# A two-block network on one core: the first block's small attention over the memory put ahead of the local one, the decays of the recurrence moved inside the attention, and v centred per head where its group norm was centred before

## The reference, cut to what matters

```python
h = rms_norm(x, norm_g)
p = h @ w_in                      # all operands of the three branches, and the gates
# branch a, a recurrence over time (8 heads of 64), with per-channel decays w and a:
#   every projection is mixed with its value one token earlier: u + mu * (u_prev - u)
#   kk = normalised k;  bonus = (sum over the head of r*k*r_k) * v
#   y = group_norm_per_head(recurrence(r, w, k, v, kk, a)) + bonus
# branch b, local attention with sinks: q, k are rms-normed per head, then rotated (rope)
# branch c, attention over 256 memory tokens: q and k rms-normed per head of 128
y_a, y_b, y_c = y * silu(z_a), local(...) * silu(z_b), cross(...) * silu(z_c)
merged = sigmoid(g0) * (y_a @ w_proj_a) + sigmoid(g1) * (y_b @ w_proj_b) + sigmoid(g2) * (y_c @ w_proj_c)
x = x + merged @ w_out
```

## Time and profile before

| | before |
|---|---|
| median of 3 runs | 1932.92 us (1932.4 to 1935.56) |
| profiled execution, its own time | 1931.05 us |
| span of its records | 1928.9 us |
| TensorE busy | 1783.4 us (92%) |
| VectorE, ScalarE, GpSimd busy | 712.4, 422.1, 136.2 us |
| mean granted clock of TensorE | 0.968 |

### The profile page before, as it was taken

How to read it: one execution, slowest core, us unless ns; L and a number is a source line. 1 busy time by engine, 2 the same in 40 slices (tenths; PEclk the granted TensorE clock), 3 DMA queues, 4 the chain that set the end, 5 groups by cost and what they waited for, 6 DMA issues and landing times.

```text
span 1928.9 us, 20481 instructions
## 1 busy us (share of the span) xinstructions
PE 1783.4 (92%) x8040; PEld 909.8 (47%) x8040; DVE 712.4 (37%) x1456; ACT 422.1 (22%) x800; POOL 136.2 (7%) x124
## 2 busy tenths in 40 slices
PE   5998789996799999999999979999999999999997
PEld 3643334452355555544454457644644444444443
DVE  3006434445533333322438988521424222221012
ACT  4022533343211111020215322400301111111000
POOL 0002120000000100000006700000000000000001
PEclk8999899998899999999999979999999999999998
DMA  4311011110001111112221112122012222221121
GB/s 181 107 66 44 33 55 44 55 44 33 33 34 35 34 34 34 34 55 95 76 76 66 66 55 66 45 77 72 27 66 77 76 76 77 76 76 66 66 87 65
DMA packets 34159, 119.75 MB, mean 62 GB/s; under 512 B 3792, under 2 KB 4048, under 8 KB 33680
## 3 DMA queue, kind: packets, MB, share of 16 engines
q1 hardware_dynamic: 32976, 113.79, 17.4%
q10 hardware_dynamic: 864, 3.35, 0.4%
q0 software_dynamic: 224, 1.31, 0.2%
HBM read 116.34 MB, written 2.10 MB: 61 GB/s over the span
## 4 chain that ended last, share of the span: by engine, by line
PE 78%; DVE 12%; issue 5%; ACT 4%; DMA 1%; POOL 0%; ACTq 0%; DVEq 0%; POOLq 0%
PE bank L462 55%; PE vpair L582 3%; PE bank L888 3%; DVE arena L1291 3%; PE bank L478 2%; PE bank L512 2%; PE opair L606 2%; DVE tmp L1282 2%; PE abank L697 2%; DVE arena L1707 2%; PE abank L555 1%; PE vpair L697 1%; DVE max L1706 1%; PE bank L487 1%; PE vpair L566 1%
## 5 line engine op out<-in xcount | busy, mean ns | idle before, releaser
L462 PE MATMUL bank<-h,ring 128*128 128x512 f32 x1840 | 835.0, 605 | 24.3 <-ACT tmp L997 14.6
L462 PEld LDWEIGHTS bank<-h,ring 128*128 128x128 f32 x1840 | 346.3, 193 | 437.2 <-issue 404.0
L462 PE MATMUL bank<-arena,ring 128*128 128x512 f32 (+1 forms) x992 | 406.0, 563 | 14.0 <-ACT arena L980 8.2
L462 PEld LDWEIGHTS bank<-arena,ring 128*128 128x128 f32 x992 | 187.8, 194 | 209.8 <-issue 184.9
L1291 DVE SCALAR_TENSOR_TENSOR x<-bank,x 128x512 f32<-128x512 f32 x32 | 22.1, 692 | 260.0 <-PE bank L462 216.7
L1291 DVE SCALAR_TENSOR_TENSOR arena<-arena,cols 128x512 f32<-128x512 f32 x125 | 94.0, 752 | 4.4
L1282 DVE TENSOR_TENSOR arena<-arena,vpair 128x256 f32<-128x256 f32 x87 | 36.6, 421 | 156.1 <-PE vpair L697 109.9
L980 ACT ACTIVATE arena<-bank 128x512 f32<-128x512 f32 (+1 forms) x67 | 34.7, 518 | 269.2 <-PE bank L462 211.1
L1285 DVE TENSOR_SCALAR arena<-arena,cols 128x512 f32<-128x512 f32 x24 | 13.1, 546 | 206.8 <-ACT arena L1246 206.6
L582 PE MATMUL vpair<-arena 128*128 128x256 f32 (+4 forms) x224 | 72.1, 427 | 7.5 <-issue 4.3
L555 PE MATMUL abank<-sq,cst 128*128 128x512 f32 (+1 forms) x58 | 33.6, 720 | 44.8 <-ACT sq L952 37.5
(11 more groups left out here) (194 smaller groups left out, 1564.0 us busy)
## 6 DMA issues: line engine op xcount, KB each, us to landing
ring<-weights SPq DMA_DIRECT2D x201, 512.0 KB, 3.2
ring<-weights SPq DMA_DIRECT2D x16, 256.0 KB, 2.9
x<-xt SPq DMA_DIRECT2D x4, 512.0 KB, 7.6
out<-h SPq DMA_DIRECT2D x8, 256.0 KB, 2.1
cst<-cst_in ACTq DMA_DIRECT2D x1, 1504.0 KB, 14.2
arena<-memt ACTq DMA_DIRECT2D x1, 1024.0 KB, 7.8
arena<-mem2t POOLq DMA_DIRECT2D x1, 1024.0 KB, 5.1
tmp<-pos ACTq DMA_DIRECT2D x1, 256.0 KB, 10.3
```

Of the source, the lines that this page charges most:

```text
L462: last = mm(o[:, 0:n], weight(), src, start=c == 0, stop=c == len(srcs) - 1)
```

## The change

The order of the first layer's work changes, and one piece of arithmetic.

- Front: the memory attention's q and both of its norms come first, beside the groups of z_c; then q, k and v of the local attention with one norm for all five tiles; then the operand tile of the decays. The z_b groups leave the front.
- Attention: memory jobs first (steps 0 to 7), then the local ones (8 to 23). What was ahead of the attention or behind it is called inside it through the new table `inject` on TensorE, `before` on ScalarE and `after` on VectorE: rotations of q after steps 1 to 4, of k after 5 and 6, kk and the decays' rounds from step 13, at 13, 16, 19 and 22. The fills are 20 groups.
- `EARLY` and `LATE` are one list `GATES`; all eight tiles are filled into the recurrence, 12 pairs for each iteration.
- v is centred per head in each decay round (one more `single`, one more VectorE product), and the four `single`s and VectorE products behind the recurrence are gone.
- Buffers follow: the decays' scratch `E` lies in xq and km, the mean squares in bb and kk.

```diff
-        lwa = thz[:, 0]
-        E = [SP[:, 0], SP[:, 1], SP[:, 2], SP[:, 3], PT[:, 0], PT[:, 1]]
+        lwa = take(T)
+        E = [xq[:, 0], xq[:, 1], xq[:, 2], xq[:, 3], km2[:, 0], km2[:, 1]]
...
-        stage("attention operands", *[A8] * (8 + 10 + 8))
-        stage("recurrence operands", *[A8] * 17)
-        stage("gates early", *[A8, V4, A8, V4] * len(EARLY))
-        stage("gates late", *[A8, V4, A8, V4] * len(LATE))
+        stage("front operands", *[A8] * (8 + 4 + 4 + 4 + 2 + 1))
+        stage("attention fill", *[A8] * (4 + 4 + 8 + 4))
+        stage("gates", *[A8, V4, A8, V4] * len(GATES))
...
+        KK_AT = 13
+        DECAY_AT = (13, 16, 19, 22)
+        GATE_PAIRS = 12
...
                     fill(work, fills(i)[2])
+                    if i in inject:
+                        inject[i]()
...
+            dense(h)
+            norm_sums(con("ones"), 4, 1, M)
+            for n in range(2):
                 dense(h)
+            work = stream([hs] * 9)
+            fill(work, 4)
+            for i in range(2):
+                norm_sums(con("ones"), 2, 1, first=2 * i)
+                fill(work, 2)
+            finish(work)
             pe.wait_ge(cst_in.sem, 16)
+            work = dense_tokens_pairs(h, NT)
+            for i in range(5):
+                fill(work, 2)
+                norm_sums(con("head_ones"), 1, 1, first=i)
+            finish(work)
+            dense(h)
+            work = stream([hs] * 20)
...
+            def bonus_sum(i):
+
                 pe.wait_ge(rk_ready.sem, i + 1)
                 single("v", con("head_ones"), E[0])
+                single("v", con("head_ones"), v[:, i, :])
+
+            inject = {}
+            for i in range(4):
+                inject[1 + i] = lambda i=i: rotate_query(i)
+                inject[DECAY_AT[i]] = lambda i=i: decay_sums(i)
+                inject[DECAY_AT[i] + 2] = lambda i=i: bonus_sum(i)
+            for s in range(2):
+                inject[5 + s] = lambda s=s: rotate_key(s)
...
+            attention(memory_jobs() + window_jobs(), work, inject=inject)
...
-                    fill(work)
+                    if it == 0:
+                        pe.wait_ge(o_read.sem, gates_from)
+                    fill(work, 2)
...
-                    fill(work)
+                    fill(work, 2)
                     pe.wait_ge(wu_ready.sem, it + 1)
...
-                    fill(work, 2)
+                    fill(work, 3)
...
-            for i in range(4):
-                pe.wait_ge(lnx_ready.sem, 1)
-                single("v", con("head_ones"), rwy[:, i, :])
             work = stream([hs] * 8)
```

On VectorE the five norms of q and k now stand right ahead of the attention, and the rounds inside it:

```diff
+            for i in range(5):
+                ri = rinv_refined(i)
+                dst = memq[:, i, :] if i < 4 else skn
+                stt(dst, dst, col("q_g" if i < 4 else "k_g"), ri, MUL, MUL, norm_applied)
+                signal_now(rope_in)
...
+            def free_scores():
+
+                st["freed"] = st["att"]
+                dve.wait_ge(exp_done.sem, st["att"])
+                signal_now(v_read)
...
                 o = v_in()
                 tt(bonus[:, i, :], o[:, :], v[:, i, :], MUL, v_read)
+                o = v_in()
+                stt(v[:, i, :], o[:, :], -1.0 / HD, v[:, i, :], MUL, ADD, v_read)
                 signal_now(head_done)
...
+            for i in range(4):
+                after[1 + i] = lambda i=i: rope_between(lambda: rope(memq[:, i, :], memq[:, i, :]))
+                after[DECAY_AT[i] + 1] = lambda i=i: decay_sums(i)
+                after[DECAY_AT[i] + 2] = lambda i=i: decay_apply(i)
...
+            after[KK_AT + 1] = first_decay
+            after[10] = lambda: dve.wait_ge(silu_done.sem, 8)
+            shifted(0)
+            dve.wait_ge(silu_done.sem, 4)
+            attention(memory_jobs() + window_jobs(), FILL1, [None] * 4 + [lambda n=n: shifted(n) for n in range(1, 13)] + [None] * 4,
+                      after=after)
```

More of the change, by code:

```diff
@@ L317, in stage_groups @@
             return groups[start[name]:start[after]]
-        RECUR = stage_groups("recurrence operands", "gates early")
-        GEARLY = stage_groups("gates early", "gates late")
+        FILL1 = stage_groups("attention fill", "gates")
         CROSSKV = [(who, n or KD) for who, n in stage_groups("cross kv", "w_out_2")]
-        GLATE = stage_groups("gates late", "gates a")
+        GATED = stage_groups("gates", "gates a")
         nblocks = sum(n for _, n in groups)
@@ L545, in take_pair, with norm_sums @@
                 return vpair if kind == "v" else opair
-            def norm_sums(ones, norms, tiles, n=T):
+            def norm_sums(ones, norms, tiles, n=T, first=0):
                 for i in range(norms):
@@ L568, in _, with attention @@
             att = {"p": 0, "pt": 0}
-            def attention(jobs, work=iter(()), fills=even_fills):
+            def attention(jobs, work=iter(()), fills=even_fills, inject={}):
                 n = len(jobs)
-                v_before.append(state["v"])
+                v_of = []
+                v_of_jobs.append(v_of)
                 for i in range(n + 3):
@@ L662, in _ @@
+            inject[7] = rotated
+            assert KK_AT == DECAY_AT[0]
+            inject[KK_AT] = first_decay
+            pe.wait_ge(wa2_in.sem, 16)
+            attention(memory_jobs() + window_jobs(), work, inject=inject)
             finish(work)
-            work = stream([hs, ybs, hs, ycs] * len(LATE))
+            ybs, ycs = ([y[:, c, :] for c in range(4)] for y in (yb, yc))
+            work = stream([hs, ybs, hs, ycs] * len(GATES))
+            gates_from = state["o"]
             n_ml = n_xx = 0
@@ L1104, in _ @@
                 do(fn(gexp[:, i, 0:7], gexp[:, i, 0:7], ACT.Exp), exps_ready)
-                read_through(reading, GEARLY, 6 * i)
-            read_through(reading, GEARLY, 24)
+            before = {KK_AT: kk_squares}
+            for i in range(4):
+                before[DECAY_AT[i] + 1] = lambda i=i: decay_tanh(i)
+                before[DECAY_AT[i] + 2] = lambda i=i: decay_exps(i)
+            attention(memory_jobs() + window_jobs(), FILL1,
+                      [lambda n=n: silu_in(yb[:, n]) for n in range(4)] + [lambda n=n: raw_tile(n) for n in range(1, 13)] +
+                      [lambda n=n: silu_in(ya[:, n]) for n in range(4)], before=before)
             act.wait_ge(head_done.sem, 4)
-            reading = {"done": 0, "todo": [gate] * (2 * len(LATE))}
+            act.wait_ge(silu_done.sem, 12)
+            reading = {"done": 0, "todo": [gate] * (2 * len(GATES))}
             act.wait_ge(o_read.sem, 24)
@@ L1783, in do @@
                 pool.wait_ge(sig.sem, sig.n)
-            dst = [y[:, n] for y in (yb, yc, ya) for n in range(4)]
+            dst = [y[:, n] for y in (yc, yb, ya) for n in range(4)]
             for n in range(12):
```

220 lines of the change are left out of this document (103 added, 117 removed).

## The result

The changed kernel takes 1873.65 us (median of 4 runs, 1872.71 to 1874.93), the kernel before 1934.24 (4 runs, 1932.4 to 1935.66): a ratio of 0.9688, interval 0.9671 to 0.9704. The forecast was 1875. The profiled execution after took 1874.93, its span 1873.1.

The account below looks back on a forecast made before the run. Chains of dependent work were taken to hold TensorE in the front and the decays, with slow clock behind each wait. -89.8 up to the recurrence, +39.3 in it and -7.5 behind gave -58, so 1875 us, range 1854 to 1901.

Parts of the forecast that it names:

- Front: Before the attention: work, 6.5 us of waits and 2 for the clock put the attention's start at 186.5, against 245.1.
- Start of the attention: At the first rotation TensorE waits 5.5 us, since VectorE must refine five tiles first.
- Step 13: In the attention, sums of kk and decays wait 1.9 us for banks from behind ScalarE's load and Ln.
- Step 16: In the attention, the scores take the bonus sum's bank, queued behind VectorE's work from step 14: TensorE waits 4.7 us.
- Later rounds: Decay rounds after the first, without kk: fill groups' readings and the bonus bank come late by 1.9, 2.2 and 0.3 us.
- The attention's total: 224.7 us of work and old waits, new waits of 5.5 + 13.1, 4 for the clock: 247.3, ending at 433.8.
- Recurrence: 24 more pairs cost 41.3 us at clock 1.00, less 2 for waits covered between iterations: +39.3.
- Behind it: Behind the recurrence, four sums go and the first gate group starts at 814.7 instead of 822.35: -7.5 us.
- rounds not hidden: Rival, chance 0.24: in the attention TensorE waits for the half rounds, 49 us instead of 13 at worst; band 1887 to 1911.
- The waits mostly do not happen: Rival, chance 0.12: the 18.6 us of waits and 6 of clock shrink to a few, 1852.
- The gate pairs: Rival, chance 0.10: pairs fill the recurrence's 15.2 us that are not busy; it grows by 26 instead of 39, 1862.
- The rule weighed: ScalarE's table switch: the skill's 1283 ns load plus about 1380 ns drain would give 1878; the forecast took 1.28 us.

Follow-up runs that it names:

- silu_ahead: The changed kernel with ScalarE reading the first z_c group ahead of Ln and Exp of the memory q tiles instead of behind them: 1866.77 us, ratio 0.9666.
- refine_inside: The changed kernel with one tile refined ahead of the attention, the other four each behind the rotations of steps 1 to 4: 1870.75 us, ratio 0.9686.
- refine_spread: The changed kernel with refining inside the attention, the second tile before the first rotation, the others each behind the rotation after it: 1867.68 us, ratio 0.9664.
- reads_first: The changed kernel with VectorE reading the sums of bonus and v ahead of the four products in each round's second half: 1867.7 us, ratio 0.9665.
- centre_outputs: The changed kernel with v left uncentred and the outputs centred behind the recurrence again, by four sums and four products: 1873.07 us, ratio 0.9685.
- three_edits: The changed kernel with refine_inside, silu_ahead and later decay rounds (13, 17, 20, 23; second halves from step 16) together: 1860.23 us, ratio 0.9634.
- four_edits: The changed kernel with refine_spread, silu_ahead, reads_first and later decay rounds (13, 17, 20, 23; second halves from step 16) together: 1858.37 us, ratio 0.9613.
- gates_behind: The changed kernel with 9 pairs per recurrence iteration as before the change, the other 24 run in one piece behind it: 1875.36 us, ratio 0.9695.

## Why the prediction was right

The mechanism was the forecast one: chains that TensorE had stood behind now lie beside its work. That the total came within 1.4 us is luck in part, since larger errors cancel in it. By steps:

- **Front.** Forecast 186.5, measured 188.1. Waits for the sums of the memory keys 2.5 us (forecast 2.6), for the third z_c group 4.31 (3.9). The 1.6 over are slow clock, sized at 2 and about 3.6: the three groups at 82.87, behind the first waits, took 22.46 us where three at 6.95 take 20.85, and 2.0 lie behind the wait of 4.31, as silu_ahead shows. The waits add 0.3, and the work was priced 0.3 too high.
- **Start of the attention.** 6.53 (5.5) at the first rotation, behind the five tiles. refine_inside and refine_spread show the cause.
- **Step 13.** Forecast 1.9, measured next to nothing: the sums of kk at 306.04 have no idle time in front, and from there to the next pair at 312.57 TensorE takes about 0.8 us more than these products cost elsewhere, in small pieces. This term was wrong. The walk took ScalarE's load to begin behind the sums, as it stood at 432.06. In the trace after, the load comes first:

```profile
304.02 1.28 ACT L996 ACT_TABLE_LOAD   x1
...
307.10 0.69 ACT L996 ACTIVATE sq<-abank,cols 128x512 f32<-128x512 f32 x1 [1.80 <-PE abank L565]
...
310.68 1.28 ACT L998 ACT_TABLE_LOAD   x1
311.98 2.98 ACT L998 ACTIVATE sq<-sq,cols 128x512 f32<-128x512 f32 x4
```

- **Step 14.** 1.32 (1.0) for the transposes, 1.42 (1.1) for the pair behind them. Right.
- **Step 16.** 3.97 (4.7). VectorE of the kernel after:

```profile
331.98 0.69 DVE L1350 SCALAR_TENSOR_TENSOR arena<-arena 128x512 f32<-128x512 f32 x1
332.71 2.15 DVE L1341 TENSOR_TENSOR arena<-arena 128x512 f32<-128x512 f32 x3
334.89 0.69 DVE L1341 TENSOR_TENSOR arena<-vpair,arena 128x512 f32<-128x512 f32 x1
335.61 0.69 DVE L1350 SCALAR_TENSOR_TENSOR arena<-vpair,arena 128x512 f32<-128x512 f32 x1
```

  The scores start at 335.63, 0.05 us behind the end of the bonus reading (334.89 + 0.69). reads_first shows it by moving that reading.
- **Later rounds.** 1.96, 1.54 and nothing, for 1.9, 2.2 and 0.3.
- **The attention's total.** It is 244.3 us long for 247.3, and the recurrence starts at 432.4 for 433.8: -91.2 for -89.8. Three errors hide in this. The new waits sum to 16.7 for 18.6. The slow clock behind them cost 7.8 for 4: 2.8 behind the first rotation, 3.3 behind step 16 and 1.7 behind the wait of 1.54, by the records. And the 224.7 of "work and old waits" was between 5 and 6 too large: it kept 2.5 us of old waits (1.01, 1.05, 0.21 and 0.20) and about 3 of slow clock at the two ends of the old attention, and of such the new one has only a wait of 0.47, at 216.27.
- **Recurrence.** 335.4 for 330.4: the largest error. The 24 pairs cost 41.2, as sized. The 2 us of covered waits never came: TensorE's waits between iterations after are those of before, to the tenth.

```profile
PE abank L735 <- DVE arena L1341: 4.2, 8, 0.5
PE vpair L827 <- DVE arena L1341: 3.2, 3, 1.1
PE vpair L725 <- DVE tmp L1341: 1.8, 3, 0.6
```

  In the trace before the lines of the same three products read 4.2, 3.2 and 1.8. The other 3 us are clock (below), which the forecast had at 1.00.
- **Behind it.** -7.6 for -7.5, but not as worked out: the group begins right at the end of the recurrence, and the price of the centring inside the attention was undersized. The working said that "its four VectorE products stand behind the bonus bank's release, so only head_done is later". It left out that its sum takes a bank of its own from the pool that the scores draw on. centre_outputs measures 9.2 us in the attention, not 3.6. Part of that was in the sum under another name: the 4.7 and 2.2 of score waits, put down to the bonus bank, are there only because the second sum shifts the scores onto it. Without them the fill pairs wait longer for ScalarE (5.1 us in rounds where the kernel after has 1.96 beside 5.5 of score waits), so that 2.4 of the 9.2 are waits, 3.6 the sums, and the rest mostly slow clock.
- **Rest.** 1093.5, unchanged within 1.2 us of before.

The errors of +1.6 in front, -3.0 in the attention, +4.9 in the recurrence, -0.1 behind it and -1.2 in the rest sum to +2.2; the profiled execution took 1874.93 for 1873. The median is nearer to the forecast's 1875 than that says, since it lies 1.3 below the profiled execution, where it was put 1.9 above; that is luck.

The rivals: rounds not hidden (1887 to 1911) needs waits over 6 us at each of the four rounds; none is over 4, and it falls. "The waits mostly do not happen" falls too, but three_edits and four_edits show what it would have been: 1860 and 1858, where 1852 was forecast. The gate pairs do not sink into the recurrence: gates_behind. VectorE is not the bound: 150.29 us busy for the 148 estimated, in 244.

**The rule weighed.** The load back for Exp starts at 310.68, takes 1.28, and the Exp follows at 311.98, 0.02 later; the load at 304.02 lay in idle time ahead of a wait. The Trainium skill (ScalarE: Activation LUTs, What ACT_TABLE_LOAD costs) adds about 1380 ns of drain to the load. No row here shows that, so the measurement decides: a switch costs 1.28 us, and ahead of a wait nothing.

## What to carry to other kernels

Chains of VectorE and ScalarE that stand alone are cheap inside a stage that has matmuls to spare: a stage of 96 us at a clock of 0.82 went, and with it 57 us of the front, for 62 us more of attention and 44 of recurrence. Look then at what each engine queues ahead of the reading that frees a bank, since one reading behind four products stops another engine's next step; and expect that moving the late work hands the lateness to the next reader unless it goes where a whole step of slack lies ahead (the attention is 0.9 us shorter in refine_inside and 6.7 in refine_spread). A part of a change that measures as nothing may be a gain and a wait that cancel: the centring was worth -0.6 us in the median with the bank wait there and 5.0 with most of it gone.

## What was not expected of the hardware

**Two lengths of the recurrence.** With the same work, kernels ran it in 332.26 to 332.29 us (six of them) or in 335.36 to 335.38 (after, silu_ahead, refine_spread), and centre_outputs in 333.8; without the added pairs it was 291.1 or 294.2 to 294.3. The kernel after has two pockets at a clock of 0.83, where the ones around have 1.00. Windows after, columns as in the earlier trace rows:

```profile
592.00:602.00 10.00, 8.35 (x127) 5.41 (x127) 5.80 (x12) 0.00 (x0) 1.35 (x2) 0.83 0.29 100
682.00:692.00 10.00, 9.02 (x106) 5.88 (x102) 6.11 (x12) 1.12 (x2) 3.92 (x5) 0.83 0.03 10
530.00:590.00 60.00, 58.08 (x698) 34.64 (x694) 17.63 (x38) 6.45 (x14) 3.92 (x5) 1.00 0.11 36
```

The waits at these places are those that stand there in every kernel, 0.4 to 1.1 us each. In windows of 10 us, silu_ahead and refine_spread have the same two pockets at the same distances from the recurrence's start, 160 and 250 us, and the six kernels of 332.3 have none. Which of the two lengths an edit far ahead brings could not be foreseen from anything in these traces, and was not settled; each kernel has one profiled execution, so it is open, too, whether the length belongs to the kernel or to the execution. It limits what a single gain under about 3 us can prove here.

**A wait can cost far more than its bracket, and the bracket does not say how much.** In the kernel after, scores, pair and transposes behind 3.97 us of waiting ran at 1.2 GHz and took 3.3 us more than at 2.4. Behind 6.53, sum, scores and pair took 2.05, 1.91 and 2.90 us for 1.02, 1.03 and 1.98. Behind only 1.54 the next pair took 3.54 (396.83), while the pairs behind the longer wait of 1.96 and behind 1.42 took 1.98, full clock. Across kernels it is the same: the pair behind 2.56 took 1.98 in three_edits and 2.59 in four_edits. So what a wait costs beyond itself could be priced here only by the run, which is why the slow clock was mis-sized in each stage.
